# Attention heads of a hybrid trunk: the two kinds of output of a pair drained two steps apart, and the next pair's first forgetting values issued one step later

## The chip, the cores and the metric

The kernel is one program on one core of a Trainium2 chip. The metric is the device time of one execution in microseconds (us); lower is better. The times below are of repeated executions, and one further execution was recorded by the hardware profiler.

## What is computed

A trunk of two layers over 528 tokens (512 and 16 learned meta tokens), width 1024, in float32. Each layer is: half a SwiGLU FFN, a token mixer, half a SwiGLU FFN. The mixer of layer 0 is attention with 8 stick-breaking heads and 8 forgetting heads of width 64; only this stage is touched by the change.

```python
# stick-breaking heads (qa, ka, va), strict = key before query
z = qa @ ka.T * scale
log_not = where(strict, log_sigmoid(-z), 0)
rest = reverse_cumsum(log_not) - log_not
a_w = where(strict, exp(log_sigmoid(z) + rest), 0)
out_sb = a_w @ va
# forgetting heads (qb, kb, vb), c = cumsum(log_sigmoid(f_logit + b_f))
s = qb @ kb.T * scale + c[query] - c[key]
p = softmax(where(causal, s, -inf))
out_fox = p @ vb
out = concat([out_sb, out_fox]) @ w_out
```

## The kernel before

**Tiling.** The heads are worked off in four pairs `hp` of two stick-breaking and two forgetting heads each. A pair has eight steps `g`: steps 0 to 3 are the first head of each kind, 4 to 7 the second, and in each head four tiles. In the stick-breaking kind tile 0 is the last 128 keys, so its matrices get wider from step 0 to 3 (144 or 176 columns up to 512); in the forgetting kind tile `s` is a block of 128 queries with 144 to 528 keys. Pair 0 is written out; pairs 1 to 3 are a loop on each engine (`steps`, `Fori(1, NH // 2)`). The order on each engine is fixed by hand. Every instruction waits for counts of semaphores.

**What a step does.** TensorE (`pe_step`): `stick_scores` (scores z of tile g, line 782 and following, into bank `g % 2` of `psum[0]`), `stick_values` of the tile three steps back (lines 865 to 870), `fox_scores` (lines 802, 806), `sticks` of the tile one step back (the cumulated sum by triangular matrices, lines 822 to 829), `fox_values` three steps back (lines 882 to 889), `turn` one step back (transposes the probabilities, lines 842 to 847). At step 3 the tile three steps back is the pair's own first one; there `stick_values` and `fox_values` stand at the end of the step instead. ScalarE (`act_step`): `act_log` (lines 1003 to 1007: abs, exp, ln), `stick_weight` one step back (line 1113, the exponential that gives the stick-breaking weights), `act_probs` (lines 1016, 1019), `act_split` (line 1026, high half of softplus). VectorE (`dve_step`): `dve_scores` (lines 1293, 1302), the running sum of softplus (1323), `fox_turned` one step back (line 1360, transposed probabilities out of PSUM), `dve_probs` (line 1337, low half of softplus; 1341, 1344, the probabilities divided by their sum). GpSimd masks softplus and weights (lines 3095, 3100).

**Outputs of a pair.** All value matmuls of a pair accumulate in `psum[3]`: bank 0 stick-breaking (`o_main[:, 0]`), bank 1 forgetting (`o_main[:, 1]`). The first 16 rows of both kinds are in a small area of `psum[1]` (`o_first`). The last tiles of pair `hp - 1` are matmuls of step 2 of pair `hp`. At the start of step 3 ScalarE copies the outputs into the high half of the output projection's operand (`o_upper`, line 1119: first rows; line 1121 twice: the kinds; counter `o_hi`), after a wait for the last `fox_values`; VectorE, at the start of its step 3, subtracts to get the low half (`o_lower`, lines 1366, 1369 twice; counter `o_split`).

**Who waits.** `stick_values(hp, 0)` and `fox_values(hp, 0)` overwrite the banks, so they wait for `o_split`: 2 counts of the 3 of the pair before, and all 3. `stick_weight(g)` waits for `stick_values(g - 2)`, whose weight buffer it overwrites (`sb_pv`). `stick_scores(g)` waits for `stick_weight(g - 2)`, whose bank of `psum[0]` it overwrites (`w_done`). `fox_scores(g)` waits for `fox_turned(g - 2)` (`pt_out`). So on ScalarE and TensorE at the end of step 3 and the start of step 4:

```python
act.wait_ge(sticks_done, c + 1); count_ge(act, sb_pv, c - 1)    # stick_weight
count_ge(pe, w_done, c - 1)                                     # stick_scores
count_ge(pe, o_split, 3 * hp - 1)                               # stick_values, g == 0
count_ge(pe, o_split, 3 * hp)                                   # fox_values, g == 0
```

After the last pair, `act_drain` and `dve_drain` do the same for pair 3, and TensorE goes on with the output projection (`out_first`, line 2576, blocks 0, 1, 2, 4, 5, 6 first, then 3 and 7, which wait for the outputs of pair 3).

Of the kernel before, what the change touches and what calls it, by code (L numbers as in the profile page):

```python
# [29 lines left out]
ACT = mybir.ActivationFunctionType  # L30
# [21 lines left out]
NH = 8  # L52
# [9 lines left out]
STEPS = 8  # L62
# [98 lines left out]
def trunk(nc, x, meta_tokens, g_ffn1, w_ffn1_in, w_ffn1_out, g_mix, g_ffn2, w_ffn2_in, w_ffn2_out,  # L161
# [5 lines left out]
    with ctx:  # L167
# [475 lines left out]
        def v_turned_out(eng, r, copy):  # L643

            kind, jt = r // QT, r % QT
            _, kn = value_tile(kind, jt)
            eng.wait_ge(vt_turned, r + 1)
            if r == QT - 1:
                eng.wait_ge(v_pad, 1)
            copy(v_tok[0:kn, kind, jt, :], v_bank(r)[0:kn, :]).then_inc(vt_odd if r % 2 else vt_even, 1)  # L650
# [75 lines left out]
        def o_tile(t, hp, kind):  # L726
            return t[:, bass.ds(hp + 4 * kind, 1), META:T].rearrange("p a t -> p (a t)")
# [6 lines left out]
        def attn_pe(pe, ph, product, out_first, sums, pair, third, fourth, X, A):  # L734
# [75 lines left out]
            def sticks(hp, g):  # L810
                e, s, c = g // 4, g % 4, STEPS * hp + g
                k0, q0, nq = stick_tile(g)
                z = z_psum(g)

                if s == 0:
                    pe.wait_ge(sp_masked, c + 1)
                    later, c0 = softplus[g % 2][:, nq:nq + META], P
                else:
                    pe.wait_ge(sp_done, c + 1)
                    pe.wait_ge(stick_ready, c + 1)  # L820
                    later, c0 = stick[:, k0 + P:T], k0 + P - q0
                nc.tensor.matmul(z[:, c0:nq], neg_ones[:, :], later, start=False, stop=True,  # L822
                                 skip_group_check=True)
                w = stick_cols(g)
                pe.wait_ge(sp_high, c + 1)
                nc.tensor.matmul(z[:, 0:w], tri_r[:, :], sp_hi[g % 2][:, 0:w], start=False, stop=True,
                                 skip_group_check=True)
                pe.wait_ge(sp_low, c + 1)
                nc.tensor.matmul(z[:, 0:w], tri_r[:, :], sp_lo[g % 2][:, 0:w], start=False, stop=True,
                                 skip_group_check=True).then_inc(sticks_done, 1)  # L830
# [43 lines left out]
            def fox_values(hp, g):  # L874
                e, s, c = g // 4, g % 4, STEPS * hp + g
                if g == 0:
                    count_ge(pe, o_split, 3 * hp)
                pe.wait_ge(pt_out, c + 1)
                q0, _ = fox_tile(g)
                own = o_main[:, 1, q0 - META:q0 - META + P]  # L880
                for b in range(s + 1):
                    mm = nc.tensor.matmul(own, head_v[e][:, 1, b, :], turned_p[s][:, b, :],  # L882
                                          start=(g == 0 and b == 0), stop=True, skip_group_check=True)
                meta_v = head_v[1][:, 1, QT - 1, :]
                if e == 1:
                    mm = nc.tensor.matmul(own, meta_v, turned_p[s][:, s + 1, :],
                                          start=False, stop=True, skip_group_check=True)
                if g == 4:
                    mm = nc.tensor.matmul(o_first[:, 1, :], meta_v, first_turned[:, :],
                                          start=False, stop=True, skip_group_check=True)  # L890
                mm.then_inc(fx_pv, 1)

            def pe_step(hp, g, first):
                v, t = before(hp, g, 3, first), before(hp, g, 1, first)
                if first and g == 0:
                    return
                if first and g == 1:
                    pe.wait_ge(top_second_out, last_p.head + 1)
                    t = None
                stick_scores(hp, g)  # L900
                if v is not None and g != 3:
                    stick_values(*v)
                if first and g == 1:
                    pe.wait_ge(drained, ph.n0 + QKV)
                    pe.wait_ge(vt_even, 2)
                fox_scores(hp, g)
                if first and g == 1:
                    for r in range(QT, QT + 3):
                        turn_v(r)
                elif first and g == 2:  # L910
                    for r in range(QT + 3, 2 * QT):
                        turn_v(r)
                if t is not None:
                    sticks(*t)
                if v is not None and g != 3:
                    fox_values(*v)
                if t is not None:
                    turn(*t)

                if g == 3:  # L920
                    stick_values(*v)
                    fox_values(*v)

            def pe_drain():
                last = NH // 2 - 1
# [35 lines left out]
        def attn_act(act, ph, split, tail, root, a_high, s23_high, s14_high, a22_high, p1_copy, u2_copy, u4_copy, X, A):  # L961
# [127 lines left out]
            def act_step(hp, g, first):  # L1089
                if first and g == 0:  # L1090
                    return
                if g == 3 and not first:
                    o_upper(hp - 1)
                act_log(hp, g)
                t = before(hp, g, 1, first)
                if t is not None:
                    stick_weight(*t)
                if first and g == 1:
                    act.wait_ge(drained, ph.n0 + QKV)
                act_probs(hp, g)  # L1100
                if first and g < 3:
                    v_turned_out(act, 5 if g == 1 else 9, copy)
                act_split(hp, g)
                if first and g == 1:
                    v_turned_out(act, 7, copy)
                if first and g > 4 and g < 7:
                    split(ph.n0 + QKV + g - 5, g - 5)
# [5 lines left out]
                nc.scalar.activation(weight[g % 2][:, 0:stick_cols(g)], z_psum(g)[:, 0:stick_cols(g)],  # L1113
                                     ACT.Exp).then_inc(w_done, 1)

            def o_upper(hp):

                wait_apart(act, fx_pv, STEPS * hp + STEPS)
                nc.scalar.activation(o_firsts(X[0], hp), o_first, ACT.Copy).then_inc(o_hi, 1)
                for kind in range(2):  # L1120
                    nc.scalar.activation(o_tile(X[0], hp, kind), o_main[:, kind, :], ACT.Copy).then_inc(o_hi, 1)

            def act_drain():
                stick_weight(NH // 2 - 1, 7)
                o_upper(NH // 2 - 1)
            steps(act, act_step, act_drain)
            n1 = ph.n0 + QKV
            nc.scalar.preload_act_table_set("sqrt_and_others")
# [8 lines left out]
        def attn_dve(dve, ph, split, tail, inverse, clear_sums, weight_sums_13, weight_sum_2, weight_sum_4, a_low, a22_low,  # L1137
# [167 lines left out]
            def dve_step(hp, g, first):  # L1305
                e, s, c = g // 4, g % 4, STEPS * hp + g
                if first and g == 0:
                    return
                if g == 3 and not first:
                    o_lower(hp - 1)  # L1310
                dve_scores(hp, g)
                if first and g < 3:
                    v_turned_out(dve, QT + 2 * g - 1, nc.vector.tensor_copy)
                if s > 0:
                    _, q1, nq = stick_tile(g - 1)
                    count_ge(dve, sticks_done, c)
                    dve.wait_ge(sp_masked, c)
                    dve.wait_ge(stick_ready, c)
                    if s == 1:
                        nc.vector.tensor_tensor(stick[:, SEQ:T], stick[:, SEQ:T], softplus[(g - 1) % 2][:, nq:nq + META],  # L1320
                                                ALU.add).then_inc(stick_tail, 1)
                        dve.wait_ge(stick_tail, 2 * hp + e + 1)
                    nc.vector.tensor_tensor(stick[:, q1:T], stick[:, q1:T], softplus[(g - 1) % 2][:, 0:nq],
                                            ALU.add).then_inc(stick_ready, 1)
                t = before(hp, g, 1, first)
                if t is not None and not (first and g == 1):
                    fox_turned(*t)
                dve_probs(hp, g)
                if first and g > 4 and g < 7:
                    split(ph.n0 + QKV + g - 5, g - 5)  # L1330

# [28 lines left out]
                nc.vector.tensor_copy(turned_p[s][:, 0:n, :],  # L1360
                                      src[:, 0:n * P].rearrange("p (b q) -> p b q", q=P)).then_inc(pt_out, 1)

            def o_lower(hp):

                dve.wait_ge(o_hi, 3 * hp + 1)
                nc.vector.tensor_tensor(o_firsts(X[1], hp), o_first, o_firsts(X[0], hp), ALU.subtract).then_inc(o_split, 1)
                for kind in range(2):
                    dve.wait_ge(o_hi, 3 * hp + kind + 2)
                    nc.vector.tensor_tensor(o_tile(X[1], hp, kind), o_main[:, kind, :], o_tile(X[0], hp, kind),
                                            ALU.subtract).then_inc(o_split, 1)  # L1370

            def dve_drain():
                fox_turned(NH // 2 - 1, 7)
                o_lower(NH // 2 - 1)

            last_p = ph.pairs[-1]
            dve_scores(0, 0)
# [1801 lines left out]
```

## Time and profile before

| | us |
|---|---|
| median of 3 runs (lowest, highest) | 1770.96 (1770.2, 1771.22) |
| profiled execution, its own time | 1771.79 |
| span of its trace | 1769.8 |
| TensorE busy in the span | 1747.5 |
| VectorE, ScalarE, GpSimd busy | 1402.1, 940.8, 65.0 |

The span is what the trace covers; the profiled execution's own time is 2.0 us longer. The steps of the four pairs lie between about 505 and 628 us of the span. An engine's busy time is the union of its instructions; those of TensorE are pipelined, and their ends are modelled, so starts are read rather than ends.

### The profile page before, as it was taken

To read this page: it belongs to the slowest core of one execution; us is meant where nothing else is said; L and a number is where in the kernel's file an instruction comes from. 1 tells how busy PE (TensorE), PEld (TensorE's weight loads), DVE (VectorE), ACT (ScalarE), POOL (GpSimd) and SP (SyncE) were. 2 spreads that over 40 slices of the span, in tenths; PEclk is the share of its full clock that TensorE was granted. 3 is DMA by queue.
4 is the path that set the end of the run, shared out by engine and by line. 5 is a ranking of instruction groups with operands and counts; after the bars stand their busy time and mean duration, and the time that the engine had idled before them with its cause. 6 is when DMAs were issued, how large, how long until landed. Compare 5 with 4: busy or idle time off the path is not lost.

```text
span 1769.8 us, 34354 instructions
## 1 busy us (share of the span) xinstructions
PE 1747.5 (99%) x13632; PEld 1695.1 (96%) x13632; DVE 1402.1 (79%) x2016; ACT 940.8 (53%) x1554; POOL 65.0 (4%) x167
## 2 busy tenths in 40 slices
PE   8999999999999999999999999999999999999998
PEld 8999999999988899999999999999999988899997
DVE  6856998779978858947998789479987688499875
ACT  5433655555568843634655545346555445266555
POOL 0000000001122202000000000000000000000000
PEclk9999999999999999999999999999999999999999
DMA  5243343336565422333333323334333323244332
GB/s 160 82 125 90 98 118 97 89 93 194 182 174 132 118 72 74 98 104 93 111 96 103 101 84 96 108 85 117 98 96 90 90 71 108 79 117 115 96 95 73
DMA packets 334389, 186.84 MB, mean 106 GB/s; under 512 B 18208, under 2 KB 324960, under 8 KB 334240
## 3 DMA queue, kind: packets, MB, share of 16 engines
q1 hardware_dynamic: 330800, 175.41, 35.5%
q0 software_dynamic: 2608, 8.72, 1.3%
q8 instruction: 106, 1.74, 0.4%
q10 hardware_dynamic: 832, 0.62, 0.1%
q14 instruction: 43, 0.35, 0.1%
HBM read 171.51 MB, written 10.82 MB: 103 GB/s over the span
## 4 chain that ended last, share of the span: by engine, by line
PE 85%; DVE 9%; issue 2%; ACT 2%; DMA 1%; SPq 1%; POOL 0%; DVEq 0%; ACTq 0%; POOLq 0%
PE pair L2619 48%; PE pair L2591 18%; PE pair L2560 8%; PE pair L2953 4%; PE pair L2606 1%; PE pair L865 1%; PE pair L882 1%; PE pair L2795 1%; DVE w_lo L2052 1%; PE pair L802 1%; DVE w_lo L2036 1%; PE pair L2828 1%; PE pair L822 1%; DVE w_lo L2047 1%; DVE w_lo L1938 1%
## 5 line engine op out<-in xcount | busy, mean ns | idle before, releaser
L2619 PE MATMUL pair<-b_hi,w_hi 128*128 128x264 f32 (+1 forms) x1464 | 416.7, 285 | 2.2 <-DVE b_lo L2187 1.6
L2619 PE MATMUL pair<-b_hi,w_lo 128*128 128x264 f32 (+1 forms) x1464 | 414.7, 283 | 0.0
L2619 PE MATMUL pair<-b_lo,w_hi 128*128 128x264 f32 (+1 forms) x1464 | 414.6, 283 | 0.0
L2619 PEld LDWEIGHTS pair<-b_hi,w_hi 128*128 128x128 f32 x1464 | 275.8, 188 | 4.4 <-issue 2.9
L2619 PEld LDWEIGHTS pair<-b_lo,w_hi 128*128 128x128 f32 x1464 | 275.9, 188 | 0.0
L2619 PEld LDWEIGHTS pair<-b_hi,w_lo 128*128 128x128 f32 x1464 | 275.5, 188 | 0.0
L1553 ACT ACTIVATE w_hi<-sums_w 128x1024 fp32r<-128x1024 f32 x188 | 198.6, 1056 | 104.1 <-PE pair L2619 61.0
L1553 ACT ACTIVATE w_hi<-raw_all 128x1024 fp32r<-128x1024 f32 (+1 forms) x188 | 158.9, 845 | 141.5 <-PE pair L2619 100.0
L2619 PE MATMUL pair<-blocks_hi,w_hi 128*128 128x264 f32 (+1 forms) x816 | 231.7, 284 | 0.8 <-ACT parts L1736 0.8
L2619 PE MATMUL pair<-blocks_hi,w_lo 128*128 128x264 f32 (+1 forms) x816 | 231.3, 283 | 0.0
L2619 PE MATMUL pair<-blocks_lo,w_hi 128*128 128x264 f32 (+1 forms) x816 | 231.2, 283 | 0.0
L2591 PE MATMUL pair<-b_hi,w_hi 128*128 128x264 f32 (+1 forms) x766 | 173.6, 298 | 0.0
L2591 PE MATMUL pair<-b_hi,w_lo 128*128 128x264 f32 (+1 forms) x766 | 173.5, 298 | 0.0
L2591 PE MATMUL pair<-b_lo,w_hi 128*128 128x264 f32 (+1 forms) x766 | 173.4, 298 | 0.0
L1938 DVE TENSOR_TENSOR w_lo<-raw_all,w_hi 128x1024 fp32r<-128x1024 f32 x117 | 142.7, 1221 | 28.1 <-ACT w_hi L1524 28.1
L1524 ACT ACTIVATE w_hi<-raw_all 128x1024 fp32r<-128x1024 f32 x117 | 121.7, 1049 | 63.6 <-PE pair L2591 58.7
L2619 PEld LDWEIGHTS pair<-blocks_hi,w_hi 128*128 128x128 f32 x816 | 153.7, 188 | 1.4 <-ACT parts L1736 1.2
L2619 PEld LDWEIGHTS pair<-blocks_lo,w_hi 128*128 128x128 f32 x816 | 153.6, 188 | 0.2
L2619 PEld LDWEIGHTS pair<-blocks_hi,w_lo 128*128 128x128 f32 x816 | 153.6, 188 | 0.0
L2047 DVE TENSOR_TENSOR w_lo<-sums_w,w_hi 128x1024 fp32r<-128x1024 f32 x94 | 114.9, 1222 | 25.7 <-ACT w_hi L1553 25.6
L2440 DVE SCALAR_TENSOR_TENSOR h<-pair,h 128x528 f32<-128x528 f32 (+1 forms) x61 | 42.9, 703 | 108.9 <-PE pair L2591 108.5
L2052 DVE TENSOR_TENSOR w_lo<-sums_w,w_hi 128x1024 fp32r<-128x1024 f32 x94 | 114.7, 1220 | 17.7 <-ACT w_hi L1553 17.7
(350 smaller groups left out, 3801.3 us busy)
## 6 DMA issues: line engine op xcount, KB each, us to landing
raw_all<-in_w_ffn_in SPq DMA_DIRECT2D x173, 512.0 KB, 4.0
raw_all<-in_w_ffn_out SPq DMA_DIRECT2D x64, 512.0 KB, 4.4
raw_all<-in_w_ffn_out SPq DMA_DIRECT2D x32, 384.0 KB, 3.6
raw_all<-in_w_attn_in SPq DMA_DIRECT2D x24, 512.0 KB, 4.8
qk_dram<-qk_hi POOLq DMA_DIRECT2D x16, 264.0 KB, 4.2
qk_dram<-qk_lo POOLq DMA_DIRECT2D x16, 264.0 KB, 3.1
raw_all<-in_w_attn_out SPq DMA_DIRECT2D x8, 512.0 KB, 4.9
sb_qq<-qk_dram SPq DMA_DIRECT2D x16, 132.0 KB
```

The lines of the kernel that those rows point to most:

```text
L802: mm = nc.tensor.matmul(sc[:, c0:c1], q[:, q0:q0 + P], k[:, c0:c1], start=q is fx_qq[e], stop=True, skip_group_check=True)
L822: nc.tensor.matmul(z[:, c0:nq], neg_ones[:, :], later, start=False, stop=True, skip_group_check=True)
L1524: nc.scalar.activation(w_hi[j][:, :], raw[j][:, :], ACT.Copy).then_inc(hi_ready, 1)
L1553: return nc.scalar.activation(dst, src, ACT.Copy)
L1938: nc.vector.tensor_tensor(w_lo[j][:, :], raw[j][:, :], w_hi[j][:, :], ALU.subtract).then_inc(lo_ready, 1)
L2047: nc.vector.tensor_tensor(w_lo[1][:, :], S23, w_hi[1][:, :], ALU.subtract).then_inc(s23_lo, 1)
L2052: nc.vector.tensor_tensor(w_lo[2][:, :], s14(p.q), w_hi[2][:, :], ALU.subtract).then_inc(s14_lo, 1)
L2440: nc.vector.scalar_tensor_tensor(hm, pair_of(OUT_BANK[m], ph.last), 0.5, hm, ALU.mult, ALU.add).then_inc(drained, 1)
L2560: mm = nc.tensor.matmul(psum[j][:, bank, c0:c0 + cols], w[j][:, blk], rhs[v][:, k, t0:t0 + cols], start=(k == 0 and w is w_hi and v == 0), ...
L2591: mm = nc.tensor.matmul(bank_of[:, bank, c0:c0 + cols], w[slot][:, blk], rhs[v][:, k, from_:from_ + cols], start=(k == 0 and w is w_hi and ...
L2619: mm = nc.tensor.matmul(dst, w[slot][:, c0 + kk * P:c0 + (kk + 1) * P], rhs(v, kk), start=(fresh and kk == 0 and w is w_hi and v == 0), st ...
L2953: mm = nc.tensor.matmul(psum[j][:, bank, c0:c0 + cols], w[j][:, blk], X[v][:, k, t0:t0 + cols], start=(k == 0 and w is w_hi and v == 0), s ...
```

## The change

The three copies of a pair's output are no longer made in one block. The stick-breaking kind and the first rows (`stick_upper`) are copied by ScalarE in step 2, between `act_probs` and `act_split`, after a wait for the last `stick_values` (`sb_pv`); the forgetting kind (`fox_upper`) after `act_split` of step 3, after a wait for the last `fox_values`. On VectorE, `stick_lower` stands where the block stood, at the start of step 3, and `fox_lower` at the end of step 3, after `dve_probs`. On TensorE `fox_values(hp, 0)` leaves the end of step 3 and is issued in step 4, between `sticks` and `fox_values(hp, 1)`. It applies to the written-out pair 0 as well. No instruction is added or taken away but one wait on ScalarE.

```diff
                 if t is not None:
                     sticks(*t)
+                if g == 4:
+                    fox_values(hp, 0)
                 if v is not None and g != 3:
                     fox_values(*v)
...
                 if g == 3:
                     stick_values(*v)
-                    fox_values(*v)
...
             def act_step(hp, g, first):
                 if first and g == 0:
                     return
-                if g == 3 and not first:
-                    o_upper(hp - 1)
                 act_log(hp, g)
...
                 act_probs(hp, g)
...
+                if g == 2 and not first:
+                    stick_upper(hp - 1)
                 act_split(hp, g)
+                if g == 3 and not first:
+                    fox_upper(hp - 1)
...
-            def o_upper(hp):
+            def stick_upper(hp):
+
+                wait_apart(act, sb_pv, STEPS * hp + STEPS)
+                nc.scalar.activation(o_firsts(X[0], hp), o_first, ACT.Copy).then_inc(o_hi, 1)
+                nc.scalar.activation(o_tile(X[0], hp, 0), o_main[:, 0, :], ACT.Copy).then_inc(o_hi, 1)
+
+            def fox_upper(hp):
 
                 wait_apart(act, fx_pv, STEPS * hp + STEPS)
-                nc.scalar.activation(o_firsts(X[0], hp), o_first, ACT.Copy).then_inc(o_hi, 1)
-                for kind in range(2):
-                    nc.scalar.activation(o_tile(X[0], hp, kind), o_main[:, kind, :], ACT.Copy).then_inc(o_hi, 1)
+                nc.scalar.activation(o_tile(X[0], hp, 1), o_main[:, 1, :], ACT.Copy).then_inc(o_hi, 1)
...
             def dve_step(hp, g, first):
...
                 if g == 3 and not first:
-                    o_lower(hp - 1)
+                    stick_lower(hp - 1)
                 dve_scores(hp, g)
...
                 dve_probs(hp, g)
+                if g == 3 and not first:
+                    fox_lower(hp - 1)
...
-            def o_lower(hp):
+            def stick_lower(hp):
 
                 dve.wait_ge(o_hi, 3 * hp + 1)
                 nc.vector.tensor_tensor(o_firsts(X[1], hp), o_first, o_firsts(X[0], hp), ALU.subtract).then_inc(o_split, 1)
-                for kind in range(2):
-                    dve.wait_ge(o_hi, 3 * hp + kind + 2)
-                    nc.vector.tensor_tensor(o_tile(X[1], hp, kind), o_main[:, kind, :], o_tile(X[0], hp, kind),
-                                            ALU.subtract).then_inc(o_split, 1)
+                dve.wait_ge(o_hi, 3 * hp + 2)
+                nc.vector.tensor_tensor(o_tile(X[1], hp, 0), o_main[:, 0, :], o_tile(X[0], hp, 0),
+                                        ALU.subtract).then_inc(o_split, 1)
+
+            def fox_lower(hp):
+
+                dve.wait_ge(o_hi, 3 * hp + 3)
+                nc.vector.tensor_tensor(o_tile(X[1], hp, 1), o_main[:, 1, :], o_tile(X[0], hp, 1),
+                                        ALU.subtract).then_inc(o_split, 1)
```

## Rows read from the trace of the kernel before

**Rows 1.** The page: TensorE's busy time; the chain that ended last, by engine.
```profile
PE 1747.5 (99%) x13632; PEld 1695.1 (96%) x13632; DVE 1402.1 (79%) x2016; ACT 940.8 (53%) x1554; POOL 65.0 (4%) x167
...
PE 85%; DVE 9%; issue 2%; ACT 2%; DMA 1%; SPq 1%; POOL 0%; DVEq 0%; ACTq 0%; POOLq 0%
```

**Rows 2.** Waits of TensorE, 510 to 632 us: us in total, times, longest.
```profile
PE pair L782 <- ACT b_rows L1113: 2.1, 5, 0.8
```

**Rows 3.** Timeline of TensorE, pair 2, steps 3 and 4: start, duration, operation.
```profile
577.42 0.49 PE L842 MATMUL pair<-ident,sq 128*128 128x128 f32 x3
577.97 0.48 PE L865 MATMUL pair<-b_rows,head_v 128*128 128x144 f32 x2
...
578.43 0.38 PE L870 MATMUL pair<-b_rows,head_v 128*128 128x16 f32 x2
578.65 0.47 PE L882 MATMUL pair<-c_room,head_v 128*128 128x128 f32 x2
579.46 0.33 PE L782 MATMUL pair<-sb_qq,sb_kk 128*128 128x144 f32 x1 [0.34 <-ACT b_rows L1113]
...
580.56 0.36 PE L802 MATMUL pair<-fx_kk,fx_qq 128*128 128x144 f32 x1
...
582.27 0.61 PE L882 MATMUL pair<-c_room,head_v 128*128 128x128 f32 x4
582.71 0.60 PE L842 MATMUL pair<-ident,qk_room 128*128 128x128 f32 x4
```

**Rows 4.** The same stretch, TensorE's weight loads.
```profile
577.94 0.30 PEld L865 LDWEIGHTS pair<-b_rows,head_v 128*128 128x128 f32 x2 [0.27 <-issue]
```

**Rows 5.** Timeline of ScalarE, pair 2, steps 2 and 3.
```profile
574.83 0.20 ACT L1016 ACTIVATION_READ_ACCUMULATOR sq<-pair,stats 128x1 f32 x1
575.31 0.54 ACT L1026 ACTIVATE qk_hi<-b_rows 128x400 fp32r<-128x400 f32 x1 [0.28 <-POOL b_rows L3100]
575.75 0.18 ACT L1119 ACTIVATE b_hi<-pair 128x32 f32 x1
575.83 1.08 ACT L1121 ACTIVATE b_hi<-pair 128x512 f32 x2
576.78 0.61 ACT L1003 ACTIVATE v_rows<-pair 128x512 f32<-128x512 f32 x1
...
578.90 0.50 ACT L1113 ACTIVATE b_rows<-pair 128x400 f32<-128x400 f32 x1 [0.18 <-PE pair L870]
...
580.21 0.63 ACT L1026 ACTIVATE qk_hi<-v_rows 128x512 fp32r<-128x512 f32 x1
```

**Rows 6.** Timeline of VectorE, pair 2, steps 2 to 4.
```profile
575.88 0.58 DVE L1337 TENSOR_TENSOR qk_lo<-b_rows,qk_hi 128x400 fp32r<-128x400 f32 x1
...
577.04 1.29 DVE L1369 TENSOR_TENSOR b_lo<-pair,b_hi 128x512 f32 x2
578.24 0.71 DVE L1293 CUSTOM_DVE_ANT_0 pair<-pair,late_mask 128x528 f32<-128x528 f32 x1
...
579.95 0.55 DVE L1360 COPY c_room<-pair 128x384 f32<-128x384 f32 x1
580.87 0.69 DVE L1337 TENSOR_TENSOR qk_lo<-v_rows,qk_hi 128x512 fp32r<-128x512 f32 x1 [0.37 <-ACT qk_hi L1026]
...
582.08 0.31 DVE L1293 CUSTOM_DVE_ANT_0 pair<-pair,late_mask 128x144 f32<-128x144 f32 x1
...
583.35 0.69 DVE L1360 COPY c_room<-pair 128x512 f32<-128x512 f32 x1 [0.60 <-PE pair L842]
```

**Rows 7.** Pair 0, TensorE, start of step 4.
```profile
521.56 0.33 PE L782 MATMUL pair<-sb_qq,sb_kk 128*128 128x144 f32 x1 [0.34 <-ACT b_rows L1113]
```

**Rows 8.** After the last step: ScalarE's copy, VectorE's subtraction, the projection's seventh block.
```profile
628.34 0.20 ACT L1119 ACTIVATE b_hi<-pair 128x32 fp32r<-128x32 f32 x1 [4.54 <-PE pair L886]
...
629.06 1.29 DVE L1369 TENSOR_TENSOR b_lo<-pair,b_hi 128x512 fp32r<-128x512 f32 x2 [0.30 <-ACT b_hi L1121]
...
632.48 0.40 PE L2576 MATMUL pair<-b_hi,w_hi 128*128 128x264 f32 x2
```

More of the change, by code:

```diff
@@ L1114, in stick_weight @@
                                      ACT.Exp).then_inc(w_done, 1)
-            def o_upper(hp):
+            def stick_upper(hp):
[3 more added lines that the diff above has]
+            def fox_upper(hp):
                 wait_apart(act, fx_pv, STEPS * hp + STEPS)
-                nc.scalar.activation(o_firsts(X[0], hp), o_first, ACT.Copy).then_inc(o_hi, 1)
-                for kind in range(2):
-                    nc.scalar.activation(o_tile(X[0], hp, kind), o_main[:, kind, :], ACT.Copy).then_inc(o_hi, 1)
+                nc.scalar.activation(o_tile(X[0], hp, 1), o_main[:, 1, :], ACT.Copy).then_inc(o_hi, 1)
             def act_drain():
                 stick_weight(NH // 2 - 1, 7)
-                o_upper(NH // 2 - 1)
+                stick_upper(NH // 2 - 1)
+                fox_upper(NH // 2 - 1)
             steps(act, act_step, act_drain)
@@ L1361, in fox_turned @@
                                       src[:, 0:n * P].rearrange("p (b q) -> p b q", q=P)).then_inc(pt_out, 1)
-            def o_lower(hp):
+            def stick_lower(hp):
                 dve.wait_ge(o_hi, 3 * hp + 1)
                 nc.vector.tensor_tensor(o_firsts(X[1], hp), o_first, o_firsts(X[0], hp), ALU.subtract).then_inc(o_split, 1)
-                for kind in range(2):
-                    dve.wait_ge(o_hi, 3 * hp + kind + 2)
-                    nc.vector.tensor_tensor(o_tile(X[1], hp, kind), o_main[:, kind, :], o_tile(X[0], hp, kind),
-                                            ALU.subtract).then_inc(o_split, 1)
+                dve.wait_ge(o_hi, 3 * hp + 2)
[5 more added lines that the diff above has]
+                                        ALU.subtract).then_inc(o_split, 1)
             def dve_drain():
                 fox_turned(NH // 2 - 1, 7)
-                o_lower(NH // 2 - 1)
+                stick_lower(NH // 2 - 1)
+                fox_lower(NH // 2 - 1)
             last_p = ph.pairs[-1]
```

## The prediction

> **What bounds the kernel now.** I read the page first: TensorE is busy 1747.5 of 1769.8 us, and it holds 85% of the chain that ended last [rows 1]. Whatever TensorE loses anywhere is lost to the end, unless a wait behind it takes the loss up. Then the waits of TensorE in the attention steps: the largest is for ScalarE's exponential of the weights (line 1113), 2.1 us in five places [rows 2]. Three of these five are the start of step 4 of pairs 1 to 3, and a fourth is that of pair 0 [rows 3, 7]. So the change works at a place where TensorE does stand still. The rows are those of pair 2; the same places in pairs 1 and 3 repeat them to 0.05 us.
>
> The timeline of step 3 tells why it stands still. TensorE starts `stick_values(0)` at 577.97; its weight load was 0.27 us idle, without a named releaser [rows 3, 4]. VectorE's block of outputs begins just before 577.04 and its two wide subtractions take 1.29 us together [rows 6], so a single one takes some 0.68 and starts 0.61 after the other; the first ends at 577.72, and this is the count for which `stick_values(0)` waits. The load follows it by 0.22 us. After that `stick_values(0)` is through at about 578.8 (line 870 starts at 578.43, two matmuls, 0.38 us) [rows 3]; ScalarE, idle 0.18 us for exactly this, starts `stick_weight(2)` at 578.90 and takes 0.50 [rows 5]; TensorE starts `stick_scores(4)` at 579.46, idle 0.34 [rows 3]. Within this chain `fox_values(0)` starts at 578.65. Four matmuls of this kind take 0.44 us from start to start (582.27 to 582.71), two take 0.22, so it is through by 578.87 and lies wholly in time in which TensorE has nothing else to do [rows 3].
>
> **The change part by part.**
>
> *`stick_upper` in front of `act_split(2)`.* In step 2 ScalarE reads its accumulator at 574.83 for 0.20 us, then idles 0.28 for GpSimd's mask and starts the split at 575.31 [rows 5]. Now two copies stand there. The last `stick_values` of the pair before is one of the first matmuls of step 2, behind its scores, so they don't wait. In the block they cost, from start to start, 0.08 (575.75 to 575.83) and half of 0.95 (575.83 to 576.78), 0.48 [rows 5]. From about 574.95 on, the split can start at 574.95 + 0.08 + 0.48 = 575.51, so 0.20 to 0.22 us later than now. `sp_lo(2)` on VectorE starts at 575.88 as soon as the split ends (575.85) [rows 5, 6]; it goes back by the same 0.22, and with it all that VectorE does up to `stick_lower`, which ends at 577.72 + 0.22 = 577.94. TensorE's `turn(2)` at 577.42 needs the probabilities from VectorE, ready about 577.2 then: it just holds. But `stick_values(0)` goes from 577.97 to 578.19 if VectorE's count is what it waits for. If the idle 0.27 is the sequencer's own, the delay is only about 0.03. I take 0.22, since the load follows the subtraction by the same 0.21 to 0.22 in all three pairs. The delay goes down the chain: `stick_weight(2)` 579.12, `stick_scores(4)` 579.68.
>
> *`fox_values(0)` out of step 3.* What it leaves is idle time, since `stick_scores(4)` waits for ScalarE in any case. Gain 0. Where it arrives, in step 4 ahead of `fox_values(1)`, TensorE has no gap (582.27, 582.71 follow without one) [rows 3]. Cost 0.22 us.
>
> *The new wait there.* It now waits for `fox_lower`, which stands behind `dve_probs(3)` on VectorE. That follows `act_split(3)`: before, the split starts at 580.21, VectorE's `sp_lo(3)` at 580.87, its last multiplication at 581.67, and the next instruction at 582.08 [rows 5, 6]. With `stick_weight(2)` 0.22 later, ScalarE reaches the split at 580.19, the mask being no longer what it waits for (`dve_scores(3)` starts 0.35 earlier, see below), so nearly the same time. `fox_lower` starts at 582.08 and ends 0.68 later, 582.76; its copy on ScalarE, behind the split (580.21 + 0.63), is over by 581.5. TensorE arrives at 582.27 - 0.05 + 0.22 = 582.44 and waits until 582.82, or up to 0.2 more if this wait is followed by as much as the one in front of `stick_values(0)` was [rows 3, 4]. I take 0.1: 582.92, a stall of 0.48. Queued behind it are `fox_values(1)` and `turn(3)`; for `turn(3)` waits VectorE's copy at 583.35, already idle 0.60 there [rows 6], then the next scores.
>
> *What VectorE and ScalarE gain.* One wide subtraction, 0.61, leaves the front of `dve_scores(3)`: it starts at 578.24 + 0.22 - 0.61 = 577.85. Before, `fox_turned(2)` (579.95, 0.55 long) let `fox_scores(4)` go at 580.56 [rows 3, 6], 0.05 us after TensorE was free. These 0.05 are the whole gain on the path. ScalarE's logarithms of step 3 come 0.75 us earlier, and `stick_weight(2)` waits for TensorE the longer. In step 4 VectorE's scores come about 0.7 later than now, into the idle 0.60 in front of 583.35 and into TensorE's own delay.
>
> By the Trainium skill (VectorE: DVE Perf Modes, The DRAIN you can't avoid) the next VectorE instruction does not start until the pipe of the one before is empty. The rows speak against this as a full duration: of the pair of subtractions the second starts 0.61 after the first, not 0.68. By that rule the sum below would be 3 x 0.07 = 0.2 us higher.
>
> *Sum.* `fox_values(1)` starts at 582.92 + 0.22 = 583.14 instead of 582.27: 0.87 us, say 0.85, for each of pairs 1 to 3. What follows is a circle TensorE, VectorE, TensorE with fixed distances, so nothing takes it up. Bounds: with no delay in front of `stick_values(0)` (0.03) and no extra behind the wait, VectorE is 0.2 earlier too: 0.58. With 0.2 behind the wait: 0.97. Pair 0 has no drain and no `o_split` wait; there only the 0.22 counts, as `fox_values(0, 0)` also stood ahead of an idle 0.34 [rows 7]. After the last pair, the copy waits 4.54 us for the last `fox_values` and VectorE ends at 629.06 + 1.29 = 630.35; the block of the projection that needs it starts at 632.48 [rows 8]. The drain may end 0.6 earlier and it brings nothing: 0. Together 3 x 0.85 + 0.22 = 2.8 us (bounds 2.0 and 3.1). The profiled execution took 1771.79, so it would take 1774.6; against the median, which is 0.8 lower, 1770.96 + 2.8 = 1773.8, or 0.16%.
>
> **The rivals.** A measurement of this kernel can tell about 0.2% (3.5 us) from no change.
>
> *A, slower by more than that: the copies on ScalarE cost their full durations.* For `stick_upper` 0.18 and 0.60 instead of 0.56 together, and the accumulator and a wait with a register in front of them: the split comes 0.5 late instead of 0.22, the probabilities are ready at 577.5, behind `turn(2)` at 577.42, and all of step 3 moves. Each of three pairs then loses 0.85 + 0.3 = 1.15, in all 3.7 us: 1774.7. It decides as soon as the split of step 2 starts later than 575.6 in the clock of rows 5. Against it: in the block the next instruction started 0.95 after the pair of copies, not 1.08 [rows 5].
>
> *B, faster: VectorE is the true clock of steps 3 to 5.* Ends of matmuls are modelled, so a busy TensorE may be waiting in truth. Then taking 0.61 us out of VectorE in front of `dve_scores(3)` pulls step 4 forward by 0.61 - 0.22 = 0.4 a pair: -1.2 + 0.2 = -1.0 us, 1770.0. For it: the start of `fox_scores(4)` right behind `fox_turned(2)`. Against it: VectorE idles 0.37 and 0.60 in this very stretch [rows 6]. Even if the whole 0.27 and 0.59 (578.87 to 579.46) of idle time went in all three pairs, that would be 2.6 us, under 0.2%.
>
> *C, nothing but a move:* `fox_lower` is in time (VectorE waits less for ScalarE in step 3 than I think) and `stick_values(0)` isn't delayed. Then 4 x 0.22 - 3 x 0.05 = 0.7 us: 1771.7. It needs VectorE through with `dve_probs(3)` by 581.6.
>
> **How the numbers follow.** Forecast 0.6, A 0.13, B 0.09, C 0.14, the rest for what I don't see (0.04). The range leaves B's end and the far end of A out: 1770.8 to 1775.0. Slower by over 0.2% (above 1774.5): A and a tenth of the rest of the weight, 0.2. Faster by over 0.2%: nothing worked out reaches it, 0.03. Within: 0.77.
>
> **What would show it.** In the trace after, pair 2: ScalarE's split of step 2 starts 0.2 us later with respect to the accumulator's read; `stick_values(0)` about 0.22 later with respect to `turn(2)`; the idle time in front of `stick_scores(4)` grows from 0.34 to about 0.55, since `fox_values(0)` no longer fills it; a new wait of TensorE for line `fox_lower` in step 4, 0.4 to 0.5 us, three times; the distance from one pair's `stick_scores(4)` to the next one's becomes some 0.85 us longer. I am wrong if there is no wait for `fox_lower`, if the split isn't delayed, or if TensorE's step 3 gets shorter; then B or C.

## The result, and the profile after

| | before | changed |
|---|---|---|
| median (lowest, highest), 10 runs each | 1772.07 (1770.2, 1774.34) | 1776.66 (1773.44, 1778.94) |
| ratio, 95% interval | | 1.0025, 1.0017 to 1.0033 |
| span of the trace | 1769.8 | 1776.7 |
| mean granted TensorE clock of the span | 0.999 | 0.997 |

The changed kernel is slower by some 4.5 us, 0.25%. The forecast was 1773.8, at most 1775.0. I had the direction and most of the places right, and the size too small: a rise of 2.8 us was forecast, 4.6 were measured.

The page of the changed kernel: TensorE is busy 5.1 us more with the same 13632 matmuls, and its share of the chain that ended last goes from 85% to 83% [rows 1], the share without a named releaser ("issue") from 2% to 3%.

```profile
PE 1752.6 (99%) x13632; PEld 1699.1 (96%) x13632; DVE 1402.4 (79%) x2016; ACT 941.9 (53%) x1554; POOL 64.9 (4%) x167
...
PE 83%; DVE 9%; issue 3%; ACT 2%; DMA 1%; SPq 0%; DVEq 0%; POOL 0%; ACTq 0%; POOLq 0%
```

That TensorE is busy longer with the same work is what the prediction had no term for. What it did have shows in the waits of TensorE, 510 to 632 us (line waited at, releaser, us in total, times, longest): the wait for ScalarE's exponential goes from 2.1 to 3.4 us [rows 2], and two waits for VectorE's subtractions are new (line 1378 is `stick_lower`, line 1384 `fox_lower`).

```profile
PE pair L782 <- ACT b_rows L1116: 3.4, 5, 0.7
...
PE pair L865 <- DVE b_lo L1378: 0.7, 3, 0.3
...
PE pair L882 <- DVE b_lo L1384: 0.2, 1, 0.2
```

The timeline of TensorE at the same place as rows 3 (pair 2, steps 3 and 4; 3.1 us later in this trace). `turn(2)` at 580.47, `stick_values(0)` at 581.20, `stick_scores(4)` at 582.69:

```profile
580.47 0.49 PE L842 MATMUL pair<-ident,sq 128*128 128x128 f32 x3
581.20 0.48 PE L865 MATMUL pair<-b_rows,head_v 128*128 128x144 f32 x2 [0.25 <-DVE b_lo L1378]
...
581.66 0.37 PE L870 MATMUL pair<-b_rows,head_v 128*128 128x16 f32 x2
582.69 0.34 PE L782 MATMUL pair<-sb_qq,sb_kk 128*128 128x144 f32 x1 [0.65 <-ACT b_rows L1116]
...
583.38 1.15 PE L865 MATMUL pair<-v_rows,head_v 128*128 128x272 f32 x2
...
585.04 1.68 PE L822 MATMUL pair<-v_rows,neg_ones 128*128 128x400 f32 x2
585.92 1.18 PE L826 MATMUL pair<-qk_hi,tri_r 128*128 128x512 f32 x1
```

From `turn(2)` to `stick_values(0)` it is now 0.73 us instead of 0.55, and `stick_scores(4)` waits 0.65 instead of 0.34 [rows 3]. So far it is as predicted. Then the matmuls themselves get long. The pair of line 822 takes 1.68 us here. One pair before, where the stretch of step 4 looks like this, it takes 0.92:

```profile
553.84 0.33 PE L782 MATMUL pair<-sb_qq,sb_kk 128*128 128x144 f32 x1 [0.65 <-ACT b_rows L1116]
...
555.43 0.92 PE L822 MATMUL pair<-v_rows,neg_ones 128*128 128x400 f32 x2
...
556.97 0.94 PE L882 MATMUL pair<-c_room,head_v 128*128 128x128 f32 x6 [0.15 <-DVE b_lo L1384]
```

The table by stretches gives the cause (columns: stretch and length, busy time of each engine, then the granted clock, DMA share, GB/s). Around step 4 of pair 2 the granted clock is 0.85 and 0.81 on average over 5 us. That is some 3.4 us at the 1.2 GHz level and the rest at 2.4. The last line is the same step in the trace of before (there 3.2 us earlier), at full clock.

```profile
575.00:580.00 5.00, 4.86 (x31) 3.91 (x29) 4.00 (x13) 4.65 (x12) 1.27 (x5) 1.00 0.28 78
580.00:585.00 5.00, 4.10 (x25) 3.49 (x24) 4.23 (x11) 3.67 (x10) 0.74 (x2) 0.85 0.49 117
585.00:590.00 5.00, 5.00 (x26) 3.71 (x26) 2.81 (x13) 2.87 (x10) 1.24 (x4) 0.81 0.59 173
...
580.00:585.00 5.00, 5.00 (x32) 4.02 (x32) 3.92 (x17) 4.09 (x14) 1.62 (x6) 1.00 0.68 194
```

Up to the last 2 us of the span the clock was down three times: here, at the same place of pair 3, and in pair 0 between 518 and 522 us, from the end of an idle 0.92 that the kernel before has too. In the trace of before it was not down once up to the last 3 us. (All 14 traces have a fall in the last 2 to 5 us of the span, when TensorE has nothing left to do; so no run of normal length shows a mean of 1.000, and 0.999 stands for no fall before that.) The two traces also differ by 1.0 us before step 0 of pair 0, by a transfer (`fx_kk`) that landed later. This has nothing to do with the change: in the second trace of the changed kernel, step 0 starts at 500.81, in that of before at 500.75.

Put together from `stick_scores(4)` of one pair to that of the next: 28.04 and 28.02 us before (551.42 to 579.46 and on to 607.48); after, 28.85 with the clock up (553.84 to 582.69), and 30.09 with one fall (582.69 to 612.78). The longer chain is 0.81 us a pair. A fall costs 1.24 on top. The two traces' spans differ by 6.9 us. Roughly, that is 2.7 of longer chain, some 3.5 of three falls, 1.0 of the transfer, less 0.2 behind the attention steps.

### The profile page after: what moved, and what is told of

Its sections match the earlier page's. It is cut to its first block, busy times and chain, and to the rows that moved or that the text cites. A ratio compares the mean times of both kernels' runs of the same rounds, so it can differ in the third digit from the quotient of the medians.

```text
span 1776.7 us, 34358 instructions
## 1 busy us (share of the span) xinstructions
PE 1752.6 (99%) x13632; PEld 1699.1 (96%) x13632; DVE 1402.4 (79%) x2016; ACT 941.9 (53%) x1554; POOL 64.9 (4%) x167
## 4 chain that ended last, share of the span: by engine, by line
PE 83%; DVE 9%; issue 3%; ACT 2%; DMA 1%; SPq 0%; DVEq 0%; POOL 0%; ACTq 0%; POOLq 0%
PE pair L2635 47%; PE pair L2607 17%; PE pair L2576 8%; PE pair L2969 4%; PE pair L2622 1%; PE pair L2811 1%; PE pair L865 1%; DVE w_lo L2068 1%; DVE w_lo L2052 1%; PE pair L882 1%; PE pair L2844 1%; PE pair L822 1%; DVE w_lo L2063 1%; DVE w_lo L1954 0%; ACT w_hi L1540 0%
```

## The experiments

All medians are of 11 runs (6 for one). The kernels ran in four groups, each beside 15 to 33 runs of the kernel before on the same chip, whose median was 1772.5 to 1773.3; "before" is below always that of the same group. Each run comes with its mean granted clock to three digits.

**Is the clock part of it, and does it follow the runs?** The changed kernel again, without an edit.

> The changed kernel once more, as the yardstick for the others of this call. Two theories of the 4.6 us by which its median lay above the kernel before. T: two parts. First a longer chain of waits, 0.85 us in each of pairs 1 to 3 and 0.22 in pair 0, 2.8 us, in every run. Second the clock: in the trace the granted TensorE clock falls from the 2.4 to the 1.2 GHz level at the start of step 4 in pairs 2 and 3, behind an idle 0.65 us, and each time some 1.9 us go; in how many pairs this happens differs from run to run. T expects times of one kernel to follow the mean granted clock: near 1773.5 at 0.999, near 1778.5 at 0.996, and a median 4 to 5 us above before. R: the chain of waits is all of it and simply longer than 0.85 a pair; the clock falls in as many places in the kernel before. R expects the two kernels' granted clocks to be the same and the difference at equal clock to be 4.5 us.

1776.88 us, 4.1 above before; ratio 1.0021 (1.0012 to 1.003). The times go with the clock. Over the 88 runs of the kernel before in the first three groups, the medians are 1771.5 at 0.999 (40 runs), 1773.4 at 0.998 (39) and 1775.2 at 0.997 (9). Of the 21 of the changed kernel (10 and 11), 1773.4 at 0.999 (1 run), 1775.4 at 0.998 (5), 1777.1 at 0.997 (11), 1778.5 at 0.996 (4). So at equal clock the change costs 2 us, and it shifts the runs by one to two steps of 0.001, each worth 1.8. A fall of 3.4 us to half is 0.001 of the span: a step is about a fall. (In the traces a fall costs 1.0 to 1.7 us, a little less than a step; what the rest is stays open.) R fails, since it wanted equal clocks. T's first part is confirmed in size only roughly: 2.0 instead of 2.8.

The kernel before loses clock too: 48 of its 88 runs are at 0.998 or lower. This fits the rise of its median from 1770.96 in three runs to 1772.07 in ten; the clocks of those ten are not on record.

**Which part of the change opens the gap?** TensorE's part alone:

```diff
+                if g == 4:
+                    fox_values(hp, 0)
...
                     stick_values(*v)
-                    fox_values(*v)
```

> The kernel before, with one part of the change: the next pair's fox_values(0) is issued in step 4; both drains stay where they were. T: the 0.22 us of matmul no longer fills the idle time in front of stick_scores(4), so 4 x 0.22 = 0.9 us of chain, and the idle stretch of step 3 grows from 0.34 to 0.56 us, near the 0.65 of the changed kernel, so the clock falls in some pairs: median 1 to 3.5 us above before, with a mean granted clock below that of before. R: 0.9 us, clock as before. No wait for the forgetting kind's subtraction should show in step 4 under either.

1774.95, 2.2 us above before; ratio 1.0013 (1.0004 to 1.0022). No run at 0.999, six at 0.998, four at 0.997, one at 0.996. The trace, pair 2:

```profile
580.99 0.33 PE L782 MATMUL pair<-sb_qq,sb_kk 128*128 128x144 f32 x1 [0.66 <-ACT b_rows L1114]
...
582.59 1.66 PE L822 MATMUL pair<-v_rows,neg_ones 128*128 128x400 f32 x2
```

The idle time is the 0.65 of the changed kernel, not the 0.56 that I had worked out: 0.22 us of matmul had hidden 0.31 of idle time. The distance from pair to pair with the clock up is 28.25 (552.74 to 580.99), 0.21 longer, as computed. So this one move opens the whole gap in front of `stick_scores(4)`, and by the runs' mean clocks (0.9975 on average, 0.9972 for the changed kernel, 0.9983 for before) it brings most of the falls.

ScalarE's part alone (`stick_upper` ahead of `act_split(2)`, `fox_upper` at the start of step 3; VectorE and TensorE as before):

```diff
+                if g == 2 and not first:
+                    stick_upper(hp - 1)
                 act_split(hp, g)
```

> The kernel before, with another part: ScalarE copies the stick-breaking kind in step 2 ahead of the split, the forgetting kind at the start of step 3; VectorE and TensorE as before. Both theories: the split of step 2 starts 0.22 us later, and stick_values(0) and stick_scores(4) with it: 3 x 0.2 = 0.6 us. T: hardly more idle time before step 4, so the clock as before, 0.5 to 1 us above before. R the same. If stick_values(0) does not move, the delay of the split is off the path, and the step of the prediction that gave it 0.22 is wrong.

1772.36, no change to be measured: ratio 1.0002 (0.9993 to 1.0011). The 0.5 to 1 us that I had expected show at most at equal clock (at 0.999, 1772.2 in seven runs against 1771.8 in fifteen). In the trace of this kernel the delay is there, 0.17 a pair: the distance is 28.21 (551.62 to 579.83), and `stick_values(0)` now names its releaser.

```profile
577.62 0.49 PE L842 MATMUL pair<-ident,sq 128*128 128x128 f32 x3
578.34 0.48 PE L865 MATMUL pair<-b_rows,head_v 128*128 128x144 f32 x2 [0.23 <-DVE b_lo L1376]
```

Of the 0.81 a pair, 0.21 and 0.17 are these two. What is left, 0.43, is the wait for `fox_lower` in step 4. The traces show it directly too. From `stick_scores(4)` to `turn(3)` it is 3.26 us before (579.46 to 582.71), 3.48 in TensorE's part alone (552.74 to 556.22) and 3.90 in the changed kernel (553.84 to 557.74):

```profile
556.22 0.60 PE L842 MATMUL pair<-ident,qk_room 128*128 128x128 f32 x4
...
557.74 0.60 PE L842 MATMUL pair<-ident,qk_room 128*128 128x128 f32 x4
```

**Is it the gap that brings the clock down?** The changed kernel with two matmuls that do no useful work, in the gap; they write to a part of PSUM that nobody reads.

```diff
                 if g == 3:
                     stick_values(*v)
+                    for _ in range(2):
+                        nc.tensor.matmul(psum[1][:, 1, 128:256], ident[:, :], ones[:, :],
+                                         start=False, stop=True, skip_group_check=True)
```

> The changed kernel, plus two matmuls of identity by ones (128 columns) behind stick_values(0) at the end of step 3, into a part of PSUM that nobody reads. They do no useful work; they only keep TensorE busy for about 0.44 of its idle 0.65 us. The chain through ScalarE's exponential is untouched. T: the clock stays at 2.4 GHz in pairs 1 to 3, and only the longer chain is left: 2.8 us above before, 1 to 2.5 us below the changed kernel, although there is more work. R: as the changed kernel or slower by up to 0.4 us.

1774.93 over ten runs, 1.95 us below the changed kernel of the same group, with more work; ratio to before 1.0013 (1.0003 to 1.0022). (One of its 11 executions took 8059.54 us; I have no explanation and leave it out. With it the median is 1775.37.) Five of the ten are at 0.999, where the changed kernel had none. In the trace the clock is not down up to the last 3 us, the matmuls of line 925 stand in the gap, and the chain is the same: 28.85 and 28.84 us from pair to pair (551.29, 580.14, 608.98).

```profile
579.12 0.38 PE L870 MATMUL pair<-b_rows,head_v 128*128 128x16 f32 x2
579.34 0.69 PE L925 MATMUL pair<-ones,ident 128*128 128x128 f32 x4
580.14 0.34 PE L782 MATMUL pair<-sb_qq,sb_kk 128*128 128x144 f32 x1
...
581.74 0.92 PE L822 MATMUL pair<-v_rows,neg_ones 128*128 128x400 f32 x2
```

The control: the same two matmuls at the end of step 6, where there is no gap (`if g == 6:` in place of `if g == 3:` for them).

> The changed kernel, with the same two idle-work matmuls as in the filled one, but at the end of step 6, where TensorE has no gap. It tells whether the clock is held by more work as such or by work in the gap. T (the gap in front of stick_scores(4)): the gap stays at 0.65 us, the clock goes on falling behind it, and the added matmuls cost 4 x 0.44 = 1.8 us on top: some 1778.5, 6 us above before, mean granted clock 0.997 as in the changed kernel. R2 (any work helps, as the share of busy time decides): clock 0.999 in half of the runs and 1777 or less. A variant of either: VectorE's wait for turn takes the matmuls up in part; then 1 us less.

1779.5 (6 runs), 6.2 above before; ratio 1.0033 (1.0021 to 1.0045), at 0.995 to 0.998. More work as such does not hold the clock; the time is 2.6 us above the changed kernel's (in another group), where 1.8 had been expected. Its trace has three falls, in pairs 0, 1 and 3, each 0.7 to 2 us behind an idle 0.65; the one of pair 1 lasts for twice as long as the others, with a whole 5 us at the lower level. The gap in the timeline, and the stretch behind it:

```profile
553.26 0.34 PE L782 MATMUL pair<-sb_qq,sb_kk 128*128 128x144 f32 x1 [0.65 <-ACT b_rows L1120]
```

```profile
555.00:560.00 5.00, 5.00 (x19) 4.15 (x18) 1.88 (x9) 2.23 (x9) 1.24 (x4) 0.50 0.59 161
```

**And the kernel before?** One such matmul at the end of its step 3, in the idle 0.34:

> The kernel before, with one idle-work matmul behind fox_values(0) at the end of step 3, 0.22 us of the idle 0.34. T: if the clock also falls behind this smaller gap in some executions of the kernel before, they become rarer: median 0 to 1 us below before, granted clock at 0.999 more often than in half of the runs. If the clock of the kernel before falls elsewhere (the idle 0.6 and 0.9 us in pair 0), nothing changes: within 0.3 us. R (clock has nothing to do with the gap): no change.

1772.46 against 1773.25, ratio 0.9998 (0.9989 to 1.0007): nothing that can be measured. Six of its eleven runs are still at 0.998, so this gap is not where the kernel before mostly loses its clock. No trace of it caught a fall.

Then both kernels with such matmuls in the gaps behind which a trace had shown a fall, or could: at the end of step 3 of each pair (one in the kernel before, two in the changed one), four between `stick_scores` and `fox_scores` of step 3 of pair 0, two at the end of step 7 of pair 0. One gap of 0.60 us, in front of `stick_scores(3)` of pair 0, stays open in both.

> The kernel before, with idle-work matmuls (identity by ones, 0.22 us each, into a part of PSUM that nobody reads) in every gap of TensorE in the attention steps behind which a trace so far showed the clock fall or could: one at the end of step 3 of each pair, four between stick_scores and fox_scores of step 3 of pair 0 (an idle 0.9 us), two at the end of step 7 of pair 0 (an idle 0.75). T: the clock stays up, the runs above 1773 vanish, median 1771 to 1771.8, 1 to 2 us below before. If the spread of the kernel before has its source elsewhere, the median stays within 0.5 us of before.

> The changed kernel with the same idle-work matmuls in the same gaps, two at the end of step 3. With both kernels' clocks held up, only the chain of waits should be between them. T: 0.81 us in each of three pairs and 0.2 in pair 0, 2.6 to 2.7 us above before_fill_all, with less than 0.7 either way, and a mean granted clock of 0.999 in nearly every run of both; 1773.6 to 1774.5. R (the chain is all of the loss): 4 us or more above before_fill_all.

1771.8 (1771.23 to 1772.7) and 1773.81 (1773.08 to 1775.24). All 22 runs are at 0.999. The wide spread of both kernels is much smaller: 1.5 and 2.2 us, where the kernel before had 3.1 in the same group and the changed one 5.5 in its first ten runs. The kernel before gains only 0.65 us by it, less than the 1 to 2 expected: at 0.999 it is at 1771.4 without the matmuls, so they cost some 0.4 us themselves. The medians are 2.0 us apart. I had expected 2.6 to 2.7, with 0.7 either way. In the two traces, from the first `stick_scores(4)` to the last it is 85.90 and 87.96 us, 2.06 more, and the last steps add 0.6; so the chain in the traces is 2.7 us longer. The difference of medians and that of the traces agree within the spread, and what the 0.7 us between them are stays open. R (4 us or more of chain) is out in either case. Filling the gaps takes 3.1 us off the changed kernel (1776.88 to 1773.81, in different groups) and 0.65 off the kernel before (in one group): the clock's share of the loss is about 2.4 us, or 2.1 if each kernel is first compared with before in its own group (4.1 less 2.0). The chain's is 2 to 2.7.

**Does the delayed split feed the falls?** The changed kernel with `stick_upper` behind the split:

```diff
-                if g == 2 and not first:
-                    stick_upper(hp - 1)
                 act_split(hp, g)
+                if g == 2 and not first:
+                    stick_upper(hp - 1)
```

> The changed kernel with stick_upper behind the split of step 2 instead of ahead of it, so that the split is not delayed. Chain: the 0.17 us by which turn(2) to stick_values(0) had grown go again, 3 x 0.17 = 0.5 us. The gap in front of stick_scores(4) stays, and the clock keeps falling: 0.3 to 0.7 us below the changed kernel, 3.5 to 4 above before. If it is more, the delayed split also fed the fall of the clock (R3).

1774.19, only 0.9 above before, where 3.5 to 4 had been expected: ratio 1.001 (1.0001 to 1.0019). The chain is as expected (28.68 us a pair, 552.02 to 580.70), the idle time is still 0.65. But five of its eleven runs are at 0.999, as large a share as of the kernel before (11 of 28), so of the 2.7 us that it gains on the changed kernel (in different groups) the greater part is clock. This speaks for R3, except that TensorE's part alone has the same idle time there (0.65 in front of `stick_scores(4)`, 0.85 in the 5 us up to it, in both) and never ran at 0.999. In the changed kernel it is 0.65 and 1.04. How often the clock falls does not follow from the gap alone. What else decides, I could not settle.

**All traces counted.** Pairs 1 to 3 of the 14 traces give 42 places in front of `stick_scores(4)`. Five traces (the changed kernel's two, TensorE's part alone, the control, the split first) have an idle 0.65 there: 15 places, the clock fell behind 6. In the nine others it is 0.34 or less: 27 places, no fall.

The length of a gap is not what decides by itself, though. In front of step 0 of pair 1, eleven of the traces have an idle 0.74 or 0.75, longer than 0.65 and with about as much idle time in the 5 us up to it (0.74 to 0.96): no fall behind any of them. The open gap of 0.60 in pair 0 had none behind it in the three traces with the other gaps filled, and 32 of those 33 runs are at 0.999.

**A version that beats both?** It keeps the early copy, and lets `stick_values(0)` go ahead of `turn(2)`, so that ScalarE's exponential can start earlier, with `turn(2)` in the gap. VectorE subtracts the stick-breaking kind in step 2.

The main edits, against the changed kernel (cut; `fox_upper` and `fox_lower` move to the start of step 3, `fox_values(0)` back to its end):

```diff
# TensorE, pairs 1 to 3
+                if g == 3 and not first:
+                    stick_values(*v)
                 if t is not None:
                     turn(*t)
...
# VectorE
                     fox_turned(*t)
+                if g == 2 and not first:
+                    stick_lower(hp - 1)
                 dve_probs(hp, g)
```

> A version meant to be faster than both. As in the changed kernel ScalarE copies the stick-breaking kind in step 2; VectorE subtracts it in step 2 too, behind fox_turned(1) and ahead of dve_probs(2); the forgetting kind's copy and subtraction stand at the start of step 3; on TensorE, in pairs 1 to 3, stick_values(0) goes ahead of turn(2), and fox_values(0) stays at the end of step 3. T: stick_values(0) is done some 0.6 us earlier, so ScalarE's exponential and stick_scores(4) are too, with turn(2) and fox_values(0) in the gap: 28.04 us from pair to pair becomes 27.4 to 27.6, 1.2 to 1.8 us in all, and with almost no idle time left before step 4 the clock falls less often: median 1.5 to 3 us below before. Against it: ScalarE's copy delays the split by 0.2 and VectorE's subtraction sp_lo(2) by 0.6, so that sticks(2) or turn(2) waits; then 0 to 0.5 us of it are lost per pair.

1772.63 against 1773.25, ratio 0.9995 (0.9986 to 1.0004), where 1.5 to 3 us had been expected. From `stick_scores(0)` to `stick_scores(4)` it took 14.19 us instead of 14.73 (566.52 to 580.71), but the second half 13.70 instead of 13.30: `fox_lower` at the start of VectorE's step 3 made `fox_turned(2)` late, and `fox_scores(4)` waited. Mended, `fox_lower` between `fox_turned(2)` and `dve_probs(3)`, `fox_values(0)` in step 4:

> The faster version, mended. In values_first the way from stick_scores(0) to stick_scores(4) became 0.54 us shorter, but the way on to the next pair 0.40 longer, since VectorE's fox_turned(2) came late behind fox_lower and fox_scores(4) waited for it. Here fox_lower stands between fox_turned(2) and dve_probs(3), where VectorE idled 0.37, and fox_values(0) of pairs 1 to 3 goes to step 4, 0.22 us of work moved out of a gap. T: 14.2 and 13.5 us instead of 14.73 and 13.30, 0.3 us a pair, 1 us in all below before at equal clock. The gap in front of stick_scores(4) is 0.2 to 0.3 us, so the clock falls no more often than before.

1771.81 against 1772.45, ratio 0.9994 (0.9985 to 1.0003); 14.19 and 13.53 us, as computed, and 1769.7 to 1770.6 in its five runs at 0.999. On VectorE, `fox_lower` (line 1388) now stands where the engine had idled for ScalarE's split:

```profile
580.85 0.55 DVE L1374 COPY c_room<-pair 128x384 f32<-128x384 f32 x1
581.32 0.68 DVE L1388 TENSOR_TENSOR b_lo<-pair,b_hi 128x512 f32 x1
581.92 0.68 DVE L1351 TENSOR_TENSOR qk_lo<-v_rows,qk_hi 128x512 fp32r<-128x512 f32 x1
```

With the matmuls of before_fill_all added:

> The mended faster version with the idle-work matmuls of before_fill_all (one at the end of step 3 of each pair, four between stick_scores and fox_scores of step 3 of pair 0, two at the end of step 7 of pair 0). T: the chain is 1 us shorter than that of the kernel before, and the clock no longer falls: all runs at 0.999, median 1770.2 to 1771.0, some 2 us (0.1%) below before. If the matmuls take as much as they give, the median is that of values_first_2, 1771.8.

1770.98 (1769.26 to 1772.93) against 1772.63, ratio 0.9991 (0.9982 to 1.0), ten of eleven runs at 0.999. The interval just reaches 1. Its median is 1.65 us below before of the same group, 0.8 below before with its gaps filled (in another group); that it is really faster is not shown beyond the noise.

## Why the prediction was wrong, point by point

- **`stick_upper` ahead of the split**: right. Accumulator read to split was to grow from 0.48 to about 0.7; in the changed kernel the read is at 577.88, the split at 578.53, 0.65. Predicted delay of `stick_values(0)` 0.22, measured 0.17 to 0.18, in two kernels. Copies count from start to start here, not with their full durations, so rival A was wrong.

```profile
577.88 0.20 ACT L1017 ACTIVATION_READ_ACCUMULATOR sq<-pair,stats 128x1 f32 x1
577.98 0.19 ACT L1122 ACTIVATE b_hi<-pair 128x32 f32 x1
578.05 0.60 ACT L1123 ACTIVATE b_hi<-pair 128x512 f32 x1
578.53 0.55 ACT L1027 ACTIVATE qk_hi<-b_rows 128x400 fp32r<-128x400 f32 x1
```

- **`fox_values(0)` out of step 3**: its cost, 0.22 in step 4, is right (0.21 measured alone). "What it leaves is idle time [...] Gain 0" is the step that failed: the term for the bare gap was put at nothing. In the chain it is true. But the matmul had another use there: it kept the gap in front of `stick_scores(4)` at 0.34 us. Bare, the gap is 0.65 (forecast: 0.55), in the five traces that have it the clock fell behind it in 6 of 15 places, and only 1 of 21 runs of the changed kernel had no fall at all, against 40 of 88 before. This was worth 2.1 to 2.4 us.
- **The new wait for `fox_lower`**: right in place and nearly in size, 0.43 against 0.48. In the trace it shows in pair 1. Where the clock is down it is covered: TensorE comes late enough. With the clock held up, in the changed kernel with all gaps filled, it shows in all three pairs. This fits that a fall costs 1.24 us in the changed kernel (30.09 less 28.85) and 1.65 in TensorE's part alone (29.90 less 28.25).
- **What VectorE gains, pair 0, the drain**: right. From the first matmul of the projection to the end it is 1141.8 us before (628.00 on) and 1141.5 after (635.17 on), so the earlier copy in the drain brought nothing.
- **The sum of the chain**: 0.85 a pair predicted, 0.81 measured; 2.8 us against 2.7 in the traces and 2.0 in the medians at equal clock.
- **The base**: I put the sum on a median of three runs at a high clock. In ten runs the kernel before lies 1.1 us higher. That alone would not have put the result into the range: 1775.0 and 1.1 are 1776.1, still below 1776.66. The range was a range of chains, and it had no term for the clock at all. The prediction had itself worked out that the gap would grow by two thirds, but no row of the trace of before showed a fall behind any gap of these steps.
- **The signs**: those that the prediction named all came (split 0.17 later, `stick_values(0)` too, a longer gap, a wait for `fox_lower`, 0.81 us a pair more). They checked the chain of waits, and none of them checked the clock.
- **The rivals**: B and C were wrong. The changed kernel did end above A's 0.2%, by a mechanism that was none of mine. The 0.2 that I gave to that side was carried by the wrong reason.

## What to carry to other kernels

In this kernel, work that stood in an idle stretch of TensorE was free only as far as the chain of waits went. Before such work is moved out, look how long the bare gap is, and whether the granted clock falls behind gaps of that length anywhere in the trace or in the runs' mean clocks. A gap elsewhere that has no fall behind it proves little: here 0.75 had none, and 0.65 had six. And compare runs at equal mean clock: it split 4.5 us into about 2 of chain and the rest of clock, which neither median nor interval does.

## What the runs showed of the hardware

- In pairs 1 to 3 the granted clock fell to the 1.2 GHz level 0.7 to 2 us behind idle stretches of only 0.65 us (with 0.2 to 0.4 us more idle time in the 5 us up to their end), and came back after some 3.4 us, in one case after 6.8, at a price of 1.2 to 1.7 us for the shorter ones. With 0.34 us it never did so there. In five of the 14 traces it also fell in step 3 or 4 of pair 0: three times within 0.1 us of the end of the idle 0.9, twice 5.5 us behind it, with 0.65 or 0.34 of idle time nearer by. Behind an idle 0.75 in front of pair 1 it never fell (eleven traces). Whether it falls at a given gap differs from run to run of one kernel.
- Two idle-work matmuls of 0.22 us each in that gap kept the clock up in it (three places of the trace, and five of ten runs at 0.999 instead of none of eleven); the same two elsewhere did not. The Trainium skill (TensorE: Matmul & The Clock Gate, A second HAM failure mode: psum-queue depth-cycling) tells of a kernel whose clock swings since TensorE frequently idles briefly between groups of matmuls. The traces here agree that short idle stretches go with falls, with an idle 0.65 us once in each such stretch as the measured case; which short stretches do, they leave open.
- With those gaps filled, the runs of the kernel before spread by 1.5 us instead of 3.1. About half of its spread from run to run is the clock.
